# Low parts of the out projection's weights made by VectorE instead of GpSimd

## The reference: what is computed

```python
def layer(x, pos, lp, cache):
    ... = project(x, pos, lp['attn_norm'], lp['w_in'], lp['gmlp_norm'], lp['mlstm_gate_b'])
    ...
    mixed = jnp.concatenate([a_out.reshape(B_, T, A_WIDTH), b_out, (c_o * c_h).astype(x.dtype)], axis=-1)
    x = x + mixed @ lp['w_out']
    y, conv_state = conv_ffn(x, lp['ffn_norm'], lp['w_up'], lp['conv_w'], lp['conv_b'], lp['w_down'], conv_buf)
    x = x + y
```

## Time and profile before

| | us |
|---|---|
| median of 3 runs | 2510.92 (2509.18 to 2513.74) |
| the profiled execution | 2508.14 |
| its span | 2506.4 |
| PE busy | 2442.9 (97%) |
| DVE busy | 1606.7 (64%) |
| ACT busy | 1095.8 (44%) |
| POOL busy | 577.7 (23%) |
| GpSimd's low parts, L1695 | 58.2 (24, into `wb`) and 19.1 (8, into `wN`) |

### The profile page before, as it was taken

The page is one execution under the profiler, slowest core; times in us unless marked ns, Lnnn a source line. Parts: engine busy times, 40 slices in busy tenths (PEclk is TensorE's granted clock), DMA queues, the critical chain, the costliest instruction groups (busy, mean ns, idle before and its releaser), DMA issues.

```text
span 2506.4 us, 41744 instructions
## 1 busy us (share of the span) xinstructions
PE 2442.9 (97%) x16499; PEld 2377.6 (95%) x16499; DVE 1606.7 (64%) x2689; ACT 1095.8 (44%) x2041; POOL 577.7 (23%) x526
## 2 busy tenths in 40 slices
PE   8999999799999999999999999997999999999998
PEld 8999888799999999999999998887999999999997
DVE  3115688788888887465611267878888888864454
ACT  6325665534333333344433356554343333333443
POOL 0001244632222220010110113446322222200111
PEclk9999999999999999999999999998999999999999
DMA  4443322112222223655524333221222222255554
GB/s 152 129 132 96 111 88 68 53 52 78 78 69 78 78 67 109 197 173 162 184 78 148 109 110 109 70 62 53 64 78 78 69 78 78 68 165 173 173 173 153
DMA packets 234902, 265.88 MB, mean 106 GB/s; under 512 B 15286, under 2 KB 207572, under 8 KB 232532
## 3 DMA queue, kind: packets, MB, share of 16 engines
q1 hardware_dynamic: 234708, 263.21, 33.1%
HBM read 213.06 MB, written 50.11 MB: 105 GB/s over the span
## 4 chain that ended last, share of the span: by engine, by line
PE 86%; DVE 4%; POOL 3%; issue 3%; ACT 2%; DMA 1%; DVEq 0%; POOLq 0%; SPq 0%; ACTq 0%
PE bank L317 26%; PE bank L319 26%; PE bank L318 26%; PE bank L968 1%; PE bank L1041 1%; PE bank L1010 1%; PE bank L1026 1%; PE bank L1051 1%; PE bank L990 1%; POOL acc L365 0%; DMA zb<-z_scratch 0%; POOL tLf L1795 0%; PE bank L1002 0%; DVE hc L2006 0%; POOL wN L1695 0%
## 5 line engine op out<-in xcount | busy, mean ns | idle before, releaser
L317 PE MATMUL bank<-actH,wb 128*128 128x384 f32 (+1 forms) x1552 | 509.1, 328 | 0.0
L318 PE MATMUL bank<-actL,wb 128*128 128x384 f32 (+1 forms) x1552 | 505.0, 325 | 0.0
L319 PE MATMUL bank<-actH,wb 128*128 128x384 f32 (+1 forms) x1552 | 504.3, 325 | 0.0
L317 PE MATMUL bank<-wzH,actH 128*128 128x256 f32 (+3 forms) x1296 | 369.9, 285 | 5.3 <-DVE wzL L1824 4.5
L319 PE MATMUL bank<-wzH,actL 128*128 128x256 f32 (+3 forms) x1296 | 364.9, 282 | 0.0
L318 PE MATMUL bank<-wzL,actH 128*128 128x256 f32 (+3 forms) x1296 | 364.5, 281 | 0.0
L317 PEld LDWEIGHTS bank<-actH,wb 128*128 128x128 f32 x1552 | 292.5, 188 | 4.9 <-issue 4.1
L318 PEld LDWEIGHTS bank<-actL,wb 128*128 128x128 f32 x1552 | 293.1, 189 | 0.5
L319 PEld LDWEIGHTS bank<-actH,wb 128*128 128x128 f32 x1552 | 293.2, 189 | 0.0
L317 PEld LDWEIGHTS bank<-wzH,actH 128*128 128x128 f32 (+1 forms) x1296 | 237.1, 183 | 7.9 <-issue 6.4
L317 PE MATMUL bank<-tH,wb 128*128 128x384 f32 x704 | 237.0, 337 | 1.2 <-ACT vn L1645 1.2
(11 more groups left out here) (289 smaller groups left out, 5211.3 us busy)
## 6 DMA issues: line engine op xcount, KB each, us to landing
raw<-in_w_up SPq DMA_DIRECT2D x88, 512.0 KB, 4.5
raw<-in_w_down SPq DMA_DIRECT2D x88, 512.0 KB, 3.6
g_scratch<-cv SPq DMA_DIRECT2D x44, 545.0 KB, 3.2
rawz<-in_w_in SPq DMA_DIRECT2D x22, 1024.0 KB, 5.5
zb<-z_scratch SPq DMA_DIRECT2D x16, 1156.0 KB, 5.5
tHf<-g_scratch SPq DMA_DIRECT2D x88, 192.0 KB, 3.6
z_scratch<-zst SPq DMA_DIRECT2D x128, 128.0 KB, 1.7
raw<-in_w_out SPq DMA_DIRECT2D x128, 128.0 KB, 2.8
```

Of the source, the lines that this page charges most:

```text
L317: pe.matmul(out, aH, bH, start=first, stop=False)
L318: pe.matmul(out, aH, bL, start=False, stop=False)
L319: return pe.matmul(out, aL, bH, start=False, stop=last)
```

## The change

The low parts of the out projection's weights move from GpSimd to DVE, with the same arithmetic. `W_LOW` gets new places: each of the twelve among the mixers is now in a place `dense(b, j)` of DVE, behind `add_x`. The four of the head go into DVE's program at four points. The semaphores and their counts stay.

```diff
-        W_LOW = {(3, 0): (0, 1), (3, 1): (2,), (4, 0): (3, 4), (4, 1): (5,), (5, 0): (6,), (5, 1): (7,), (6, 1): (8,),
-                 (7, 0): (9, 10), (7, 1): (11,)}
+        W_LOW = {(3, 2): 0, (3, 3): 1, (3, 7): 2, (4, 2): 3, (4, 3): 4, (4, 7): 5, (5, 3): 6, (5, 7): 7, (6, 7): 8, (7, 3): 9,
+                 (7, 5): 10, (7, 7): 11}
...
-                def split_out(k):
-                    h, lo = wide(k)
-                    pool.wait_ge(wo_h, l * N_WO + k + 1)
-                    pool.tensor_tensor(lo, raw(k % 2), h.bitcast(F32), ALU.subtract).then_inc(wo_l, 1)
-
                 def adds(b, late):
...
-                    if (b, late) in W_LOW:
-                        for k in W_LOW[b, late]:
-                            split_out(k)
...
                 norm_add(pool, n, 1, 7)
-                split_out(12)
-                split_out(13)
                 norm_power(pool, n, 1)
-                split_out(14)
-                split_out(15)
...
+                def split_out(k):
+                    h, lo = wide(k)
+                    dve.wait_ge(wo_h, l * N_WO + k + 1)
+                    dve.tensor_tensor(lo, raw(k % 2), h.bitcast(F32), ALU.subtract).then_inc(wo_l, 1)
+
                 def dense(b, j):
...
                     if (b, j) in Z_LOW:
                         split_wz(Z_LOW[b, j])
+                    if (b, j) in W_LOW:
+                        split_out(W_LOW[b, j])
...
                 norm_diag(dve, n, 0)
+                split_out(12)
+                split_out(13)
                 add_out(0)
...
                 add_out(2)
+                split_out(14)
                 dve.wait_ge(row_mm, row_at(n, 1) + 1)
                 for k in range(KT):
                     scaled(actF[:, k, C1], 1, k)
+                split_out(15)
                 add_out(3)
```

## The result

The changed kernel takes 2518.5 us (median of ten runs, 2515.9 to 2522.9) against 2511.2 us before (median of ten, 2507.9 to 2517.8): +7.2 us by the medians. The ratio is 1.0031 with a 95% interval of 1.0021 to 1.004, that is +7.8 us, between +5.3 and +10.

The account below looks back on a forecast made before the run. PE was busy 2442.9 of 2506.4 us, so only its idle time or slow clock could be won or lost. Terms -2.2 + 3.2 + 1.1 + 3.4 = +5.5 us on the 2510.9 median gave 2516.4, range 2509.5 to 2521.5.

Parts of the forecast that it names:

- SP's queue: Mixers: zb loads issued later behind w_out, which waits for DVE's low parts at (b, 7); +1.1 us, bounds 0 to +5.
- Block 7: Mixers, block 7: PE's waits at L938 and L1067 go as GpSimd's splits stop stretching DVE; -2.2 us in all.
- New wait at (6, 1): Start of block 6: PE waits 1.9 us per layer for weight 7's low part on DVE; net +3.2 us.
- The head: Head of up phase: split 15 behind eight `scaled` issues w_up's second half 2.1 us later; +1.7 per layer, +3.4.
- Clock left as it is: PE's mean granted clock, 0.88 of full speed in the head, was assumed unchanged; no term in the sum.
- Rival A: Faster: DVE's chain paces the mixers, so PE's waits there empty; -5.2 us, 2505.7; chance 0.10.
- Rival B: No difference: w_up's 2.1 us delay is absorbed, so the head adds 0; 2513 us; chance 0.22.
- Rival C: Slower still: zb behind w_out on SP costs about +3 more per layer in two mixer blocks; 2522 us; chance 0.18.

Follow-up runs that it names:

- mixers_k7_early: Kernel before with the mixers' twelve low parts on DVE, weight 7's at (5, 6), 2, 5 and 8 still at (b, 7); 0.0 us against before.
- k7_alone: Kernel before with only weight 7's low part moved from GpSimd to DVE's place (5, 7); +3.3 us against before.
- head_only: Kernel before with only the head's four low parts on DVE, at the places of the change; +3.0 us against before.
- mixers_only: Changed kernel with the head's four low parts put back on GpSimd, the mixers' twelve staying on DVE; +7.0 us against before.
- mixers_early: Kernel before with the mixers' twelve low parts on DVE, 2, 5, 7 and 8 at (b, 6), head's on GpSimd; -0.3 us against before.
- k7_early: Changed kernel with weight 7's low part one place earlier, at (5, 6) instead of (5, 7); +2.5 us against before.
- mixers_early_sq3: mixers_early with ACT's square for GpSimd's third head sum moved ahead of the w_up conversions; 2507.5 us, -3.0 us against before.

## Why the prediction came out right, step by step

The forecast was +5.5 us with +3.5 to +8 for its own case, measured are +7.2 (by ratio +7.8), so slower by more than 0.2%. Sign, size and the two largest terms are right; one term, SP's queue, is nearly four times what was forecast in the profiled execution, whose touched stretches add 9.1 us and not 5.5. By the medians the parts fit the whole: mixers_k7_early 0.0, k7_alone +3.3 and head_only +3.0 make +6.3 of the +7.8. Only mixers_only does not fit: 0.0 and +3.3 would make +3.3, and it stands at +7.0.

- **Block 7, -2.2.** Right. The waits at L938 and L1067 are gone, and the lag falls by 1.2 and 1.3 us there; it falls by the same 1.3 from L1026 to L1067 in every version with the mixers' splits on DVE.
- **New wait at (6, 1), +3.2.** Right in place and length (1.86 per layer, 1.9 forecast), and by the times in the releaser, which the profile doesn't name. The 0.3 us to come back at L1026 of block 6 came back as 0.1 in one layer and not at all in the other, so the term is +3.7. k7_alone measured it by itself at +3.3 (+1.0 to +5.5).
- **SP's queue, +1.1.** The late zb is in the trace, the size failed: the bound was right, the value taken inside it too low. zb went out at 322.8 in before's time, 322.6 was forecast. The rope was to end at 331.5 and ended at 332.3. For this there are two reasons. The transfer took 7.5 us from issue to rope and not up to 6.7; the "up to 1 us" for the tail of 512 KB was a guess that no row stood behind, and the profiles show 5.6 to 7.5. And the prediction counted the contention that goes, but not the one that comes: DVE's new split at (4, 2) meets the rope. In mixers_k7_early zb did take 6.7 us, and its rope still ended at 332.3 in before's time. That made the L1026 wait 1.5 us longer, where 0.7 stood in the sum, and then the clock fell, which stood nowhere: 1.58. With 0.6 and 0.5 in block 5 the term is 4.2 us in this execution, near the upper bound of 5. By the medians it is smaller: mixers_k7_early, with block 7's -2.5 in it, stands at 0.0, which leaves some +2.5 for this term, within 2.8; and it stands only 0.3 above mixers_early, whose zb is not behind w_out. No run says how often it is large.
- **The head, +3.4.** Right at +3.9 in the profile (+1.4 and +2.5) and +3.0 by head_only, though in layer 1 by two errors that cancel, which is luck: w_up's second half came 2.7 us later and not 2.1 (split 15 began at 470.0 in before's time, forecast 469.4, as four DVE subtractions in front took 2.64 instead of 1.96 us beside GpSimd's sum), and the relief was 1.2 us and not 0.4 (the sum 0.89 instead of 1.81, `xw` 3.64 instead of 3.95). 2.7 - 1.2 = 1.5 against 1.4 seen. In layer 2 they did not cancel: w_up's second half came 3.3 us later, for its transfer took 4.6 us from issue to ACT's conversion and not 4.0 as before. The first head wait was forecast at 7 to 8 us and was 8.4 and 9.2.
- **Clock left as it is.** Right in the head for the two layers together, not for each (0.83 and 0.90 before, 0.90 and 0.84 now), and wrong in block 4.
- **Rival A** (DVE paces the mixers, the L1026 waits vanish) fell: with the stretching of `hc` gone they grew, 2.6 to 4.8 us in layer 1 and 1.6 to 3.3 in layer 2. DVE being free earlier did not start ACT earlier. **Rival B** fell with head_only. **Rival C** happened once, in block 4 of layer 1, L1026 at 2.4 us; in layer 2 none is above 1.3.

What stays open: mixers_only costs 7.0 us by median, where weight 7's wait (3.7) and block 7's gain (-2.5) leave 1.2 and the late zb something. mixers_k7_early, the same kernel without that one wait, costs nothing. So the wait of 3.7 us seems to cost 7 in this company and 3.3 alone. The intervals (2 to 3 us each way) and the different chips allow half of that to be chance. The granted clock that is on record for every execution points at PE's clock: 0.990 or 0.991 in the three faster executions of mixers_only, 0.988 or 0.989 in six of the eight slower ones, but 0.990 in the other two. By an estimate, 0.002 of 2515 us is 5 us of PE's full speed, as much as parts the two groups. In k7_alone it is 0.990 to 0.992 in the four faster ones and 0.988 to 0.990 in the seven slower ones. Where in the kernel the clock was lower in them, and whether a wait was the cause, no profile shows: that of mixers_only was of the three faster ones.

## What to carry over

Before a step is moved to a faster engine, look at what that engine waits for in front of it, and who needs the step's product next. Here a subtraction of half the duration became a wait of 1.9 us per layer because it was queued behind an addition that waits for PE, and one place earlier it costs nothing. Work taken off an engine that idles for another (GpSimd, 3.3 us idle for ACT's square, then 9.9) wins nothing, and contention taken away in one place comes back where the two engines next meet: when you count the stretching that goes, look also at what the moved step will run beside in its new place.

## What the runs showed of the hardware that was not expected

PE's clock fell to its lower level in eight places among the mixer blocks, in six of the profiles. Seven of them stand behind an L1026 wait, of 2.4 us (changed kernel, k7_early and mixers_k7_early, block 4 of layer 1), 1.9 (mixers_k7_early, block 4, and k7_early, block 5, of layer 2), 1.4 (mixers_only, block 3 of layer 2) and 1.25 us (mixers_early_sq3, block 4 of layer 2), and cost 1.5 to 1.6 us each. The eighth, in k7_alone, stands behind waits of 0.50 and 0.59 us. So the length of a wait does not decide it: the clock fell behind every L1026 wait of 1.9 us or more, but not behind one of 1.67 (mixers_early_sq3, block 3 of layer 2), nor behind waits of 1.25 and 1.26 us in the same block 4 of layer 2 of four other profiles, nor behind the wait of 1.6 us at (6, 1) in any profile that has it. What else decides was not tested.

Four DVE instructions with both operands in SBUF took 1.96 us alone and 5.24 to 5.64 us beside GpSimd's; four of GpSimd took 3.64 to 5.56 us. Neither side is spared. And a short GpSimd instruction that met a split of DVE's in block 4 ended 0.37 to 0.39 us after it, in four profiles, whenever it had begun.
